# VectorE's rows of a first-product step: all but one moved from the step's end to ahead of its wait for the gelu

## What is computed

```python
s1, i1 = lax.top_k(s[:, :, 0], 16); s2, i2 = lax.top_k(s[:, :, 1], 16)
...
idx = ...                             # 8 heads x 16 experts per token
gates = jax.nn.softmax(top_s)
u_rows = peer_u[idx]
act = gelu(einsum('phkd,pd->phk', u_rows, x))
out = einsum('phk,phkd->pd', gates * act, peer_v[idx])
```

## Time and profile before

| | before |
|---|---|
| median of 3 runs | 4890.27 us (4867.7 to 4891.28) |
| the profiled execution | 4882.34 us |
| its span (first to last instruction) | 4880.4 us |
| TensorE's granted clock, mean of the span | 0.906 of full speed |
| TensorE matmul busy | 3994.8 us, 82% |
| VectorE busy | 2811.9 us, 58% |
| GpSimd busy | 1976.3 us, 40% |
| ScalarE busy | 1292.6 us, 26% |

### The profile page before, as it was taken

The page is one execution under the profiler, slowest core; times in us unless marked ns, Lnnn a source line. Parts: engine busy times, 40 slices in busy tenths (PEclk is TensorE's granted clock), DMA queues, the critical chain, the costliest instruction groups (busy, mean ns, idle before and its releaser), DMA issues. The chain is left out here.

```text
span 4880.4 us, 64794 instructions
## 1 busy us (share of the span) xinstructions
PE 3994.8 (82%) x24202; PEld 3585.6 (73%) x24202; DVE 2811.9 (58%) x4458; ACT 1292.6 (26%) x1794; POOL 1976.3 (40%) x1138
## 2 busy tenths in 40 slices
PE   8997989999986989775888888888888776666667
PEld 2225888888875979774888887888888776666656
DVE  0006654555553238978676776776777675454555
ACT  1004334333431132232333222222222221111112
POOL 0003222222223333243666666665666664343442
PEclk9998999999986999888999999999999998878778
DMA  7781212222221222233999999999999996666763
GB/s 286 290 296 52 92 61 75 76 74 77 74 80 43 99 106 78 72 124 143 362 358 358 377 366 348 371 372 344 373 386 375 362 358 247 250 242 250 262 233 144
DMA packets 288840, 1090.61 MB, mean 223 GB/s; under 512 B 24200, under 2 KB 77704, under 8 KB 220296
## 3 DMA queue, kind: packets, MB, share of 16 engines
q1 hardware_dynamic: 203152, 543.60, 30.5%
q0 software_dynamic: 73728, 536.90, 28.6%
q10 hardware_dynamic: 11776, 7.52, 0.5%
HBM read 1047.54 MB, written 40.40 MB: 223 GB/s over the span
## 5 line engine op out<-in xcount | busy, mean ns | idle before, releaser
L246 POOL TENSOR_TENSOR wlo<-raw,whi 128x1024 fp32r<-128x1024 f32 x551 | 1333.2, 2427 | 1700.9 <-ACT whi L242 1695.0
L242 ACT CAST whi<-raw 128x1024 fp32r<-128x1024 f32 x672 | 695.8, 1051 | 1677.7 <-DMA raw<-in_u 452.7
L261 PE MATMUL gps<-hi_d,whi 128*128 128x320 f32 x2048 | 689.3, 337 | 320.4 <-POOL wlo L246 319.1
L2042 PE MATMUL gps<-chi,whi 128*128 128x320 f32 x2048 | 682.2, 333 | 236.5 <-POOL wlo L246 144.3
L261 PEld LDWEIGHTS gps<-hi_d,whi 128*128 128x128 f32 x2048 | 424.3, 207 | 345.9 <-POOL wlo L246 343.9
L261 PE MATMUL gps<-lo_d,whi 128*128 128x320 f32 x2048 | 674.3, 329 | 0.0
L261 PE MATMUL gps<-hi_d,wlo 128*128 128x320 f32 x2048 | 673.0, 329 | 0.0
L2042 PE MATMUL gps<-clo,whi 128*128 128x320 f32 x2048 | 668.0, 326 | 0.0
L2042 PE MATMUL gps<-chi,wlo 128*128 128x320 f32 x2048 | 666.0, 325 | 0.0
L2042 PEld LDWEIGHTS gps<-chi,whi 128*128 128x128 f32 x2048 | 417.7, 204 | 261.3 <-issue 192.7
L2129 DVE SCALAR_TENSOR_TENSOR dps<-ring,coef,dps 128x2048 f32<-128x2048 f32 x252 | 591.8, 2349 | 3.1
(11 more groups left out here) (381 smaller groups left out, 5888.0 us busy)
## 6 DMA issues: line engine op xcount, KB each, us to landing
raw<-in_u SPq DMA_DIRECT2D x256, 512.0 KB
raw<-in_v SPq DMA_DIRECT2D x256, 512.0 KB
wada<-in_w_ada SPq DMA_DIRECT2D x24, 4096.0 KB, 12.8
raw<-in_w_in SPq DMA_DIRECT2D x96, 512.0 KB
gateD<-gst SPq DMA_DIRECT2D x8, 2560.0 KB, 7.5
gate<-gateD SPq DMA_DIRECT2D x32, 640.0 KB
raw<-in_w_out SPq DMA_DIRECT2D x32, 512.0 KB
raw<-in_w_q SPq DMA_DIRECT2D x32, 512.0 KB
```

The source lines that it names most:

```text
L242: act.copy(whi[:, k.slot, :], raw_of(k)).then_inc(W.hi, 1)
L246: pool.tensor_tensor(wlo[:, k.slot, :], raw_of(k), whi[:, k.slot, :].bitcast(F32), ALU.subtract).then_inc(W.lo, 1)
L261: m = pe.matmul(gps[:, bank, 0:DT], w, x[:, kt, :], start=(kt == 0 and n == 0), stop=(kt == KT - 1 and n == 2))
L2042: m = pe.matmul(gps[:, 2 + dt, 0:DT], w[:, slot, cols], x[:, buf, c, :], start=(c == 0 and n == 0), stop=(c == NG - 1 and n == 2))
```

## The change

In a step of A on VectorE, the rows of the step but one (1 or 2) stood behind `rest` and the `wlo` that VectorE makes; they now stand ahead of the wait for the step's gelu. The one row between `gated` and `rest` stays. No instruction is added or removed, and no other engine's program is changed.

```diff
                     def A(g, buf, k, after):
                         for c in range(NG):
                             due = rows_due((g - 2) // 2, g % 2 * NG + c)
+                            for _ in range(due - 1):
+                                take()
                             dve.wait_ge(S.gel, g * NG + (c + 1))
                             gated(g, c, gps[:, c % 2, 0:DT])
                             take()
                             rest(g, buf, c, gps[:, c % 2, 0:DT])
                             for j in (2 * c + 2, 2 * c + 3):
                                 lo(k.plus(j) if j < 8 else after.plus(j - 8))
-                            for _ in range(due - 1):
-                                take()
```

## The result

The changed kernel takes **4525.57 us** (median of 4 runs, 4524.26 to 4529.21) against 4886.34 for the kernel before (four runs now, one more than in the table above): a ratio of 0.9269, 95% interval 0.9243 to 0.9295. The forecast was 4660, the range 4580 to 4790. The direction and the circle in A were right; the time lies 54 us under the range. The profiled execution took 4529.21 us, span 4527.3, so 353 us of span are to be found.

A forecast was written before the change was run, and what follows sets the result against it. It took transfers to bound the fast part and a fetch, row, gelu and product circle the slow part; gains 159 + 20 + 44 = 223 us from the profiled 4882 gave 4660 us, range 4580 to 4790.

The forecast's parts named there:

- the circle in A: Five-tile ring: GpSimd's fetch precedes `wlo` and waits for a row behind the gelu, which waits for TensorE; 112.6 us a group.
- the chain of 5.9, 6.1 and 9.5 us: Steps of A with five tiles: after the gelu's start, row done at 5.9, fetch off 0.3 later, TensorE at 9.5.
- The first term: A(25) to A(31), steps of A with five tiles: three steps fall from 49.7 to 27 us; gain 159, ends 134 and 169.
- my allowance for fuller transfers (27): Steps of A with five tiles: 27 us taken for three, between ends of 25.6 and 30.5 with transfers nearly full.
- the floor of the transfers in the early groups: 23 fast groups: at 388 GB/s, 66.5 or 72.7 us a group; gain 44 us, ends nothing and 103.
- Rival 3: Transfers reach their floor in the fast part and A its better end: gain 299, time 4583; chance 0.10.
- Rival 1: Fast part gains nothing, its transfers already being the bound: time 4703; chance 0.22.
- the way from A to the next A: Six times with five tiles, last gelu of A to next first: 62.9 us falls by 3.4 each, 20 in all.
- The pause ahead of B: TensorE's 7.12 us pause ahead of B(25), for `wlo` behind a fetch: fetch freed, `clo` left; gain 3.4 us each.
- rival 2: Clock stays low in A, TensorE at 1.2 GHz: three steps take 38.4 us, gain 99, time 4783; chance 0.14.
- rivals 4 and 5: 4 (0.05): five-tile rows land late, 4860 to 4890. 5 (0.03): rows ahead of A's first gelu wait for data, slower.
- The cover of A's first gelu: VectorE's idle time left ahead of A's first gelu, 2.7 to 6.1 us, hides the moved rows at no cost.

The follow-up runs named there:

- the move in the first step alone: Kernel before, with the rows moved only in the first step of each A: 4801.24 us, ratio 0.9826.
- the later steps: Kernel before, with rows moved from A's second step on and none ahead of A's first gelu: 4655.08 us, ratio 0.9521.
- The move in the last step alone: Kernel before, with the rows moved only in the last step of each A: 4806.49 us, ratio 0.9849.
- the changed kernel with five rows fetched: Changed kernel, with GpSimd starting with five rows fetched in place of six: 4570.42 us, ratio 0.9368.

## Why the prediction was wrong, and where it was right

**The circle was right, with its numbers.** The order on VectorE within A, the place in the ring from which the slow part starts, and the chain of 5.9, 6.1 and 9.5 us were read from the code and the earlier trace rows, and the trace after has them to a tenth. Two steps of A(27) take 16.9 us, inside the 15.9 to 17.1; the product that doesn't wait takes 7.0, where I had estimated 6.4. The first term, 159 us, came out at 168, inside its ends: three steps take 25.5 us on average, next to the 25.6 of A(11) before, and my allowance for fuller transfers (27) was not needed.

The upper ends of the terms add up to 299 us, and 353 were measured. Of the 54 between, 16 lie in the early groups, 34 between A and the next A, and the rest mostly behind A(31), where I had no term.

**What failed first: the floor of the transfers in the early groups**, with 44 us taken, 103 at most, and 119 measured. I took 388 GB/s, the best 100 us of the trace before, for what the transfers can do, and the distance to it, 103 us, for the upper end. That window's share was 0.99, so it looked full; but the same trace has stretches of 4 us with more, two of them here:

```profile
3067.50:3071.50 4.00, 4.00 (x30) 4.00 (x29) 3.67 (x4) 0.00 (x0) 1.96 (x2) 1.00 1.02 415
3071.50:3075.50 4.00, 3.37 (x23) 3.10 (x22) 0.00 (x0) 1.03 (x1) 0.88 (x1) 1.00 1.03 419
```

The changed kernel has 395 over 1000 us and 406 over 100. The 16 groups of `u` rows now take 65.4 us, under the "floor" of 66.5. And 2 us a group, the idle DMA time at A's first gelu, was the wrong place to look: a row there is worth 9 us in all or nothing (the move in the first step alone), the later steps 71. Rival 3, which had this part at its floor, came nearest, at 4583. Rival 1 (no gain here) is refuted. The figure of about 358 GB/s from the Trainium skill, DMA: Bandwidth & Descriptors, section "Where 436 GB/s comes from", which stood beside it, is no bound in this kernel, which moved 395. From 363 to 395 GB/s the DMA share rose only from 0.95 to 0.99; why the same bytes also take less of the engines' time stays open.

**What failed second: the way from A to the next A, 3.4 us a group, 20 in all.** It measured 61. B's pauses inside did stay, at 2.99, but two other things were wrong.

The pause ahead of B fell further than I said. I left `clo` there, ready 3.6 us behind A's last gelu. But B(25), which follows A(26), multiplies the result of A(25), whose `clo` is long done. In the changed kernel TensorE starts B(25) at 4033.37, 2.2 us behind A(26)'s last gelu at 4031.21, and VectorE makes A(26)'s `clo` only after that:

```profile
4034.33 0.48 DVE L2143 TENSOR_TENSOR clo<-gps,chi 128x320 fp32r<-128x320 f32 x1
```

TensorE's pauses of over 0.6 us between A and the next A add up to 117 us before, over the six, and to 82 after: 35 us of the 61.

The other 26 are the clock. Over the six, 334 matmuls ran at the lower level before and 114 after; there a matmul starts 0.27 us behind the one before it, at the upper level 0.147. With a pause of 7.1 us ahead of it, each B of the kernel before starts at the lower level, and in B(25) the clock falls again in every later pair. I had "less time at the lower clock" as the upper end, 27 us, together with the pause, and had not worked it out for all of B. The prediction gave no account of when the clock stays up, and the runs give none: B(25) of the changed kernel starts at the upper level behind a pause of 2.19 us and keeps it, while B(26), behind one of 2.30, and B(24), behind one of 0.75, start at the upper level too and lose it. The move in the last step alone gives 8 of the 10.2 us a group, some 6 of it pauses.

**The rivals about the other side.** No clock of one half in A: 0.93 to 1.00 there (rival 2). No wait of VectorE in that part ends with a row's landing, and the moved rows end 2.5 us ahead of the gate (rivals 4 and 5). The cover of A's first gelu, 2.7 to 6.1 us by the prediction, was thus enough, by 2.5 us in A(27).

## What to carry to other kernels

When two engines run the same hand-written program with a ring between them, write down for each wait which instruction of the other engine it stands for, and what that one is queued behind; here one ring tile less turned a wait for the row behind a gelu into a wait for the row behind the next, and 38 us a group hung on it (112.6 with five tiles, 74.9 with six). Moving the instruction, starting the producer one place later, or giving back the tile each break the circle, and the cheapest to try is one number. When a stage is to be freed from a bound, don't take the best long window of the bound trace for the next bound: look at its best short stretches too. Check for each wait that is left which group's result it is for, and price the stages behind the changed one at both levels of the clock.

## What the runs showed of the hardware

Pauses of about 3 us in every second step of B go with a granted clock of 1.00 through all of B(25) in the changed kernel, and with 0.86 to 0.87 in its last three pairs before, where 11 or 12 of 48 matmuls run at the lower level each time. The changed kernel's own B(24), with the same pauses, goes through both. What decides between the two stays open.

VectorE's subtraction of two SBUF tiles took 5.55 us in place of 1.22 when GpSimd had started the first of two subtractions of its own 0.2 us earlier. In the trace of the changed kernel with five rows fetched, 43 of its 44 instructions of this line that start while a subtraction of GpSimd is running take over 1.5 us, and none of the other 79 does. The Trainium skill, SBUF — State Buffer, section "Who interferes with whom", says that a VectorE instruction with two SBUF inputs contends with a GpSimd instruction that reads SBUF, and that the one that comes second is blocked. The trace agrees; the row instructions, with one input in PSUM, kept their 2.28 and 2.35 us all through.
